# Large SBUF tiles start at multiples of 256 bytes in a two-block transformer kernel

## The reference

```python
def swiglu(x, w_gate, w_up, w_down):
    return (jax.nn.silu(x @ w_gate) * (x @ w_up)) @ w_down

h = h + 0.5 * swiglu(rmsnorm(h, ffn1_norm[l]), ffn1_w_gate[l], ffn1_w_up[l], ffn1_w_down[l])
u = rmsnorm(h, mix_norm[l])
(fq, fk, fv, ff, dq, dk, dv, iq, ik, iw, mq, g) = jnp.split(u @ w_in[l], SPLIT_POINTS, axis=-1)
```

## The kernel before

| tiles | address mod 256 | mod 64 |
|---|---|---|
| raw, w_hi, w_lo, hT, const, ones_r, zero_r, rowmax | 128 | 0 |
| cos1, sin1, iw_tok | 0 | 0 |
| ident_r, masks_r, gain, negmax | 160 | 32 |
| work, shift, u_hi, u_lo, hid_*, x_tok, q, k, v, p tiles, oT, out_tok | 96 | 32 |

## Time and profile before

### The profile page before, as it was taken

How to read it: one execution, slowest core, us unless ns; L and a number is a source line. 1 busy time by engine, 2 the same in 40 slices (tenths; PEclk the granted TensorE clock), 3 DMA queues, 4 the chain that set the end, 5 groups by cost and what they waited for, 6 DMA issues and landing times.

```text
span 2288.6 us, 25848 instructions
## 1 busy us (share of the span) xinstructions
PE 2094.9 (92%) x9037; PEld 1648.5 (72%) x9037; DVE 1050.1 (46%) x1347; ACT 494.6 (22%) x888; POOL 1137.1 (50%) x664
## 2 busy tenths in 40 slices
PE   7999999778689899798999999999899689999996
PEld 5888887467477677686778888876677457888884
DVE  4333420555675638876533333017866434333103
ACT  2111000332233422242121110003366321111001
POOL 3666665354133145403656666664455235666661
PEclk9999999899799999999999999999999889999998
DMA  4333223222021123201323333333100012333330
GB/s 133 92 97 95 92 92 84 74 67 71 20 65 41 34 56 84 82 1 48 91 83 92 92 93 99 92 87 88 56 1 1 19 55 83 93 98 94 92 92 37
DMA packets 259801, 163.74 MB, mean 72 GB/s; under 512 B 30380, under 2 KB 249582, under 8 KB 259614
## 3 DMA queue, kind: packets, MB, share of 16 engines
q1 hardware_dynamic: 258080, 157.90, 23.7%
q10 hardware_dynamic: 1662, 5.06, 0.6%
HBM read 160.81 MB, written 2.13 MB: 71 GB/s over the span
## 4 chain that ended last, share of the span: by engine, by line
PE 80%; DVE 13%; ACT 3%; issue 2%; POOL 1%; DMA 0%; ACTq 0%; POOLq 0%; DVEq 0%; SPq 0%
PE bank L634 16%; PE bank L636 16%; PE bank L635 16%; PE bank L694 5%; PE bank L693 5%; PE bank L695 5%; PE bank L655 3%; DVE work L1639 2%; PE bank L755 2%; DVE work L1569 1%; DVE rowmax L1600 1%; PE bank L1013 1%; PE bank L1014 1%; PE bank L1015 1%; PE bank L798 1%
## 5 line engine op out<-in xcount | busy, mean ns | idle before, releaser
L565 POOL TENSOR_SCALAR w_hi<-raw 128x1024 fp32r<-128x1024 f32 x298 | 322.0, 1081 | 1023.3 <-PE bank L636 764.9
L567 POOL TENSOR_TENSOR w_lo<-raw,w_hi 128x1024 fp32r<-128x1024 f32 x298 | 745.3, 2501 | 24.9
L634 PE MATMUL bank<-u_hi,w_hi 128*128 128x512 f32 x1632 | 686.1, 420 | 42.3 <-DVE u_lo L1513 19.0
L635 PE MATMUL bank<-u_lo,w_hi 128*128 128x512 f32 x1632 | 650.5, 399 | 0.0
L636 PE MATMUL bank<-u_hi,w_lo 128*128 128x512 f32 x1632 | 650.3, 398 | 0.0
L634 PEld LDWEIGHTS bank<-u_hi,w_hi 128*128 128x128 f32 x1632 | 309.9, 190 | 145.3 <-issue 50.2
L635 PEld LDWEIGHTS bank<-u_lo,w_hi 128*128 128x128 f32 x1632 | 310.5, 190 | 86.6 <-issue 18.3
L636 PEld LDWEIGHTS bank<-u_hi,w_lo 128*128 128x128 f32 x1632 | 310.0, 190 | 75.1
L693 PE MATMUL bank<-hid_hi,w_hi 128*128 (+1 forms) x480 | 189.8, 396 | 0.0
L694 PE MATMUL bank<-hid_lo,w_hi 128*128 (+1 forms) x480 | 189.8, 396 | 0.0
L695 PE MATMUL bank<-hid_hi,w_lo 128*128 (+1 forms) x480 | 189.8, 396 | 0.0
(11 more groups left out here) (416 smaller groups left out, 2667.2 us busy)
## 6 DMA issues: line engine op xcount, KB each, us to landing
raw<-in_w_in SPq DMA_DIRECT2D x52, 512.0 KB, 3.7
raw<-in_ffn_w_gate SPq DMA_DIRECT2D x44, 512.0 KB, 3.7
raw<-in_ffn_w_up SPq DMA_DIRECT2D x44, 512.0 KB, 3.7
raw<-in_ffn_w_down SPq DMA_DIRECT2D x44, 512.0 KB, 3.4
raw<-in_w_gate SPq DMA_DIRECT2D x22, 512.0 KB, 3.7
raw<-in_w_up SPq DMA_DIRECT2D x22, 512.0 KB, 3.7
raw<-in_w_down SPq DMA_DIRECT2D x22, 512.0 KB, 3.5
raw<-in_w_branch SPq DMA_DIRECT2D x12, 512.0 KB, 3.3
```

The costliest lines, as they stand in the source:

```text
L565: pool.tensor_scalar(w_hi[:, s, :], raw[:, k, :], 1.0, 1.0, ALU.mult, ALU.mult).then_inc(hi_done, 1)
L567: pool.tensor_tensor(w_lo[:, s, :], raw[:, k, :], w_hi[:, s, :].bitcast(F32), ALU.subtract).then_inc(split_ready, 1)
L634: pe.matmul(outs[:, 0:n], wh, rhs_hi[:, c, :], start=(c == 0), stop=False)
L635: pe.matmul(outs[:, 0:n], wh, rhs_lo[:, c, :], start=False, stop=False)
```

## The change

The starting address is rounded up to 256 bytes instead of 64, and once more before work is placed. `place` itself still rounds sizes to 32 bytes, and nothing else is edited.

```diff
--- before.py
+++ after.py
@@ -89,7 +89,7 @@
             return ctx.enter_context(nc.semaphore(name))
 
 
-        top = [(nc.sbuf_base + 63) // 64 * 64]
+        top = [(nc.sbuf_base + 255) // 256 * 256]
 
         def at(name, shape, addr, dt=F32):
             return nc.alloc_sbuf_tensor_at(name, shape, dt, offset=addr)
@@ -122,6 +122,7 @@
         negmax = place("negmax", [P, 2, TT])
         sink = place("sink", [P, HEADS])
         best8 = place("best8", [P, TT, 8])
+        top[0] = (top[0] + 255) // 256 * 256
         work_at = top[0]
         work = place("work", [P, 10, S])
         W = [work[:, i, :] for i in range(10)]
```

## The result

| kernel | median us | runs | ratio to before, 95% interval |
|---|---|---|---|
| before | 2291.82 | 4 (2290.86 to 2296.82) | |
| changed | 2252.32 | 4 (2251.76 to 2254.06) | 0.9825 [0.9808, 0.9842] |

The changed kernel is 39.5 us faster, 1.75%; its profiled execution took 2254.06 us with a span of 2252.2 us. All of its lines from L125 on stand one line lower than in the kernel before.

The account below looks back on a forecast made before the run. The prediction took TensorE's matmuls to bound the kernel (80% of the chain, 66% in the three-product panels). All terms were taken as 0, so it forecast 2291.5 us, with a range of 2275 to 2304.

Parts of the forecast that it names:

- The bound: Whole kernel: TensorE's matmuls hold 80% of the chain that ended last, the nine matmul lines of the three-product panels 66%.
- the sum's outer terms: Terms outside TensorE: 0 from GpSimd, 0 +- 3 us from VectorE and ScalarE, 0 +- 1.8 us from transfers.
- the landings: Weight transfers arriving in SBUF: 0 in the steady stretches, being hidden; 1.5 us either way at the start.
- The moving operand: Data streamed by TensorE's 512-column matmuls: at most 0.02 us a matmul or 130 us to recover, taken as 0.
- rival 2: Panels: the streaming rate depends on the moving operand's own residue; in full 2161 us; chance 0.12, little at full size.
- The line through zero: Matmul cadences at 256, 384 and 512 columns: no fixed cost per operand, only a rate paid per column left.
- Two residues give one time: TensorE's stationary operand: weight loads at residues 128 and 96 take 0.19 us and 189 ns, so 0.
- Rival 3: Panels: weights and data at one phase meet; each 1 ns beyond cover costs 6.5 us, 7 ns gives 2337 us; chance 0.06.
- a fifth for the panels: Weight transfers: a 512-byte piece at 128 costs 20 beats instead of 16, a fifth less once aligned, but hidden.

Follow-up runs that it names:

- the alternating groups: TensorE alone, blocks' computation left out, residues alternating from matmul to matmul: (0,0) with (32,32) 232.8 ns, (32,0) with (0,32) 230.7 ns.
- the grid: TensorE alone, 24 matmuls a group, all pairs of residues 0 to 224 by 32: 227.5 ns at distance (moving less stationary residue) 0, 229.2 at +64, 233.1 at -32.

## Why the prediction was wrong

**The bound and the sum's outer terms were right.** TensorE's panels set the end, and GpSimd, ScalarE, VectorE and the landings came out at 0 as reasoned: each row within 2 ns or 0.01 us of the one before, landings 0.1 to 0.2 us shorter and hidden. That transfers are hidden is confirmed from both sides: the ring alone at 0 (panels in 3.7 us) is slow, the split tiles alone with raw at 128 (3.8 us) is fast.

**The moving operand was the step that failed.** It was called the open term, bounded at 0.02 us a matmul, and set to 0. It measured 6.4 us over 960 matmuls, 6.7 ns each. The chance of 0.12 on rival 2 had the right place (the cadence of the panels) and a third of its full size of 130 us came, which put the time 23 us under the range; but the rival named the wrong variable, since the moving operand at 96 is as fast as at 0. Three readings led there:

1. *"Nor do the cadences depend on how the two operands lie to each other."* It compared -32 in a panel with one pair at distance 0 in the attention, 0.23 with 0.24 us, in a view of hundredths. The effect is 0.0067 us. The same trace has 16 such pairs (q2al,a_k0h and then q2ah,a_k0l) at full clock, from 226 to 234 ns apart and 229.7 in the mean, so one pair could have shown anything. Such a pair also stands next to `shift` with ones_r, at a distance of -32, and the alternating groups show that mixed neighbours can cost 4 ns and more; how much they cost here is not shown. The cadence over hundreds of matmuls, which was used only for the bound, was the view with the resolution.
2. *The line through zero.* 0.11, 0.17 and 0.23 us for 256, 384 and 512 columns were taken to leave only a rate. But the effect is 6 ns at 512 columns and not there at 384 or 256, so the widths without it could not speak for the width with it.
3. *"Two residues give one time"* for the weight load was true (190 and 189 ns) and is still true. The load's own time says nothing of the cadence of the matmuls beside it.

**Rival 3 had the variable and the wrong sign.** It said that weights and data at one phase would meet, and that 128 against 96 keeps them apart. At one phase they are fastest. Its argument against, the loads at 189 ns, was again the wrong row.

**What the runs say to the rules that were cited.** The Trainium skill, page "TensorE: Matmul & The Clock Gate", section "Step-by-step: what each phase is for", says that loading the next weights does not steal read bandwidth from the running matmul, through two independent ports. In this case moving the weight tiles alone changed the cadence of the matmuls by 6.7 ns, so at 512 columns the matmuls do not run free of where the weights lie; whether read bandwidth is what the two share, no run here shows.

The Trainium skill's rule on 16-byte lines (page "SBUF — State Buffer", cited in the prediction) made this term 0. At a distance of 16, where every operand still begins on such a line, the cadence was 231.7 ns, not 226.7.

The Trainium skill's rule on transactions of 256 bytes (page "DMA: Bandwidth & Descriptors", cited in the prediction) gave a fifth for the panels. With raw at 0 the feed-forward's panels landed in 3.6, 3.6, 3.6 and 3.7 us (four kernels), at 128 in 3.7, 3.8 and 3.8, at 96 in 3.8: at most 0.2 us of a transfer, and hidden. The 22 half panels of w_in, 256 KB in pieces of 256 bytes, show it more clearly: 3.3 us with raw at 0 (four kernels), 3.6 or 3.7 us in the other four.

## What to carry to other kernels

Where TensorE streams 512 float32r columns back to back with a new weight block each time, give the stationary and the moving tiles the same address against multiples of 256 bytes; here it was worth 1.75% for no work. The common value did not matter: 0 and 96 did in the kernel, all eight multiples of 32 in the grid. Before calling a rate the same in two places, read it over a hundred instructions at one width, with neighbours of the same kind, and state the smallest difference the view can show. An experiment that puts both tiles on an equally odd address is what tells "aligned" from "alike".

## What the runs showed that was not expected

- Steady float32r matmuls of 512 columns on full granted clock took 226.7 to 228.7 ns at a distance of 0, 227.0 at -16 bytes, 229 at +64, 232 to 234 at the other multiples of 32 and 239.7 at 20; no distance reached the 213 ns that half the low-clock cadence gives. At the low clock the matmuls of both kernels take 427 ns.
- 384 columns took 173 to 174 ns and 256 columns 118 to 119 ns at distances 0, +64 and -32 alike; 128 columns took 109.5 ns at 0 and 112 at the other two.
- Alternating the residue of one operand from matmul to matmul, with the other fixed, cost 231 to 234.5 ns, more than a fixed distance of +64.
